# Hybrid two-layer trunk on one core: fewer diagonals ahead of the heads' square, one more attention level read by ScalarE, three convolution taps on TensorE, and the first norm's weights spread by TensorE

## The reference

```python
h = rmsnorm(x, ln1_w[l])
z = h @ w_in[l]                       # q, k, v, g, gate rank 16, ca, cb
o = gla_chunked(q * 64**-0.5, k, v, log_sigmoid(gate) / 16)   # 4 heads
o = rmsnorm(o, gla_norm_w) * silu(g)
u = causal_dwconv(ca * sigmoid(cb), conv_w, conv_b)  # 31 taps, 512 channels
u = silu(layernorm(u, cn_w, cn_b))
x = x + concat([o, u]) @ w_out[l]
h = rmsnorm(x, ln2_w[l])
x = x + (swiglu(h) if l == 0 else moe_swiglu(h))     # dense, then top 2 of 8
```

## Time and profile before

| what | value |
|---|---|
| median of the runs | 1262.99 us |
| the profiled execution's own time | 1263.23 us |
| its span (first to last instruction) | 1261.1 us |
| TensorE busy | 1220.4 us (97%) |
| VectorE busy | 1009.9 us (80%) |
| ScalarE busy | 815.5 us (65%) |
| mean granted TensorE clock | 0.993 of full |

### The profile page before, as it was taken

How to read it: one execution, slowest core, us unless ns; L and a number is a source line. 1 busy time by engine, 2 the same in 40 slices (tenths; PEclk the granted TensorE clock), 3 DMA queues, 4 the chain that set the end, 5 groups by cost and what they waited for, 6 DMA issues and landing times.

```text
span 1261.1 us, 16917 instructions
## 1 busy us (share of the span) xinstructions
PE 1220.4 (97%) x6868; PEld 1048.5 (83%) x6868; DVE 1009.9 (80%) x956; ACT 815.5 (65%) x725; POOL 58.9 (5%) x76
## 2 busy tenths in 40 slices
PE   8997999999999899999999999999999999999996
PEld 7986899999899678788888888888888888888875
DVE  5998475544579967888888888888888888888987
ACT  5854554443366645677777777777777777777775
POOL 4000000000000000000000000000000000000000
PEclk9999999999999998999999999999999999999999
DMA  9940465656536136999999999999999999999980
GB/s 278 351 133 17 151 196 173 198 174 194 167 134 235 51 123 240 355 368 365 375 388 366 378 384 367 382 383 365 380 385 363 376 388 364 381 385 359 396 319 35
DMA packets 182381, 360.11 MB, mean 286 GB/s; under 512 B 8926, under 2 KB 68636, under 8 KB 182300
## 3 DMA queue, kind: packets, MB, share of 16 engines
q1 hardware_dynamic: 178124, 343.77, 76.4%
q0 software_dynamic: 4176, 15.21, 3.2%
HBM read 351.09 MB, written 7.86 MB: 285 GB/s over the span
## 4 chain that ended last, share of the span: by engine, by line
PE 85%; DVE 9%; issue 2%; ACT 2%; SPq 1%; DMA 1%; DVEq 0%; ACTq 0%
PE YB L1838 17%; PE WBS L1817 13%; PE WBS L1819 12%; PE WBS L1818 12%; PE YB L1492 5%; PE WBS L1423 4%; PE WBS L1425 4%; PE WBS L1424 4%; DVE acc L924 3%; DVE w_lo L863 2%; PE YB L1829 2%; PE YB L1475 2%; PE YB L1853 2%; PE WBS L1581 1%; DMA raw<-in_w_in 1%
## 5 line engine op out<-in xcount | busy, mean ns | idle before, releaser
L863 DVE TENSOR_TENSOR w_lo<-raw,w_hi 128x2048 fp32r<-128x2048 f32 x324 | 736.8, 2289 | 110.1 <-ACT w_hi L533 107.5
L533 ACT ACTIVATE w_hi<-raw 128x2048 fp32r<-128x2048 f32 x324 | 617.1, 1916 | 144.9 <-PE YB L1838 62.1
L1817 PE MATMUL WBS<-w_hi,t_hi 128*128 128x512 f32 (+1 forms) x768 | 290.2, 378 | 1.8 <-DVE w_lo L863 1.8
L1819 PE MATMUL WBS<-w_hi,t_lo 128*128 128x512 f32 (+1 forms) x768 | 285.9, 372 | 0.0
L1818 PE MATMUL WBS<-w_lo,t_hi 128*128 128x512 f32 (+1 forms) x768 | 285.4, 372 | 0.0
L1817 PEld LDWEIGHTS WBS<-w_hi,t_hi 128*128 128x128 f32 x768 | 144.7, 188 | 26.7 <-issue 2.0
L1819 PEld LDWEIGHTS WBS<-w_hi,t_lo 128*128 128x128 f32 x768 | 144.6, 188 | 25.8
L1818 PEld LDWEIGHTS WBS<-w_lo,t_hi 128*128 128x128 f32 x768 | 144.8, 189 | 24.2
L1423 PE MATMUL WBS<-t_hi,w_lo 128*128 128x256 f32 x448 | 127.4, 284 | 0.0
L1424 PE MATMUL WBS<-t_hi,w_hi 128*128 128x256 f32 x448 | 126.8, 283 | 0.0
L1425 PE MATMUL WBS<-t_lo,w_hi 128*128 128x256 f32 x448 | 126.7, 283 | 0.0
(11 more groups left out here) (296 smaller groups left out, 1382.2 us busy)
## 6 DMA issues: line engine op xcount, KB each, us to landing
raw<-in_we_gate SPq DMA_DIRECT2D x88, 1024.0 KB, 6.7
raw<-in_we_up SPq DMA_DIRECT2D x88, 1024.0 KB, 6.9
raw<-in_we_down SPq DMA_DIRECT2D x88, 1024.0 KB, 6.8
raw<-in_w_in SPq DMA_DIRECT2D x20, 1024.0 KB, 5.9
raw<-in_wd_gate SPq DMA_DIRECT2D x11, 1024.0 KB, 5.5
raw<-in_wd_up SPq DMA_DIRECT2D x11, 1024.0 KB, 5.3
raw<-in_wd_down SPq DMA_DIRECT2D x11, 1024.0 KB, 4.9
raw<-in_w_out SPq DMA_DIRECT2D x8, 1024.0 KB, 8.0
```

The costliest lines, as they stand in the source:

```text
L533: act.activation(w_hi[:, hi_slot(n), :], raw[slot][:], ACT.Copy).then_inc(hi_ready, 1)
L863: dve.tensor_tensor(w_lo[slot][:], raw[slot][:], w_hi[:, hi_slot(n), :].bitcast(F32), ALU.subtract).then_inc(lo_ready, 1)
L1817: pe.matmul(bank, xs_hi[:, k0 + k, :], hi[:, k, :], start=start, stop=False)
L1819: ins = pe.matmul(bank, xs_lo[:, k0 + k, :], hi[:, k, :], start=False, stop=stop)
```

## The change

1. **Diagonals.** ScalarE makes 7 diagonals before the heads' square where it made 13, so the rest is made after it.
2. **Level 3** (blocks of 16) is read out by ScalarE, in 8 instructions of 16 partitions, after the high part of unit 13; VectorE's two instructions go. Levels 4 to 8 are read by one VectorE instruction each, which spans both banks.
3. **Taps.** `BY_VECTOR` goes from 27 to 24: three taps per layer move to TensorE, which now has 38. It makes 15 rather than 14 between the heads' outputs and the transposes, and 7 rather than 5 after them.
4. **First norm.** GpSimd's queue fetches one row of weights; TensorE spreads it over 128 partitions as a product with a row of ones into PSUM, VectorE reads it there. Fewer unread products precede it. GpSimd clears `lnw` afterwards.
5. **Router.** The first quarter of the logits is made between the two halves of the last output product.

```diff
-        COARSE, FINE = 3, 6
-        COARSE_READS = [2, 4, 8]
+        COARSE, FINE = 4, 5
+        COARSE_READS = [2, 4, 8, 16]
...
-        BY_VECTOR = 27
+        BY_VECTOR = 24
...
-                if t == 0:
-                    sp.dma_start(lnw[:], ln1_w[0].partition_broadcast(P)).then_inc(first_lnw_ready, 16)
...
+
+            pool.dma_start(lnw[0:1, :], ln1_w[0:1, :]).then_inc(first_lnw_ready, 16)
...
+                if l == 0:
+                    pool.wait_ge(first_lnw_spread, 2)
+                    pool.memset(lnw[:], 0.0).then_inc(pads_ready, 1)
...
+                coarse(3)
                 diagonals(3)
                 decays(7)
...
-                diagonals(13)
+                diagonals(7)
...
-                if t == 0:
-                    dve.wait_ge(lnw_ready if j else first_lnw_ready, 16 * max(j, 1))
-                dve.scalar_tensor_tensor(out=h[:, t, :], in0=X[:, t, :], scalar=rstd[:, t:t + 1], in1=lnw[:],
+                if j == 0:
+                    dve.wait_ge(first_lnw_spread, 2)
+                elif t == 0:
+                    dve.wait_ge(lnw_ready, 16 * j)
+                weights = lnw[:] if j else YB[:, 2:4, :].rearrange("p a c -> p (a c)")
+                dve.scalar_tensor_tensor(out=h[:, t, :], in0=X[:, t, :], scalar=rstd[:, t:t + 1], in1=weights,
...
-                        dve.wait_ge(level_read, 2 * (FINE * l + n - COARSE))
-                    for r in range(2):
-                        bank = YB[:, 2 * (n % 2) + r, :]
-                        ins = dve.copy_predicated(att[:, r], masks[:, n - 1:n, :].broadcast_to([P, 2 * TT, P]),
-                                                  bank.rearrange("p (a i) -> p a i", i=P))
-                        ins.then_inc(level_read, 1)
+                        dve.wait_ge(level_read, FINE * l + n - COARSE)
+                    bank = 2 * (n % 2)
+                    dve.copy_predicated(att[:].rearrange("p r a i -> p (r a) i"), masks[:, n - 1:n, :].broadcast_to([P, 4 * TT, P]),
+                                        YB[:, bank:bank + 2, :].rearrange("p r (a i) -> p (r a) i", i=P)).then_inc(level_read, 1)
...
-                level_read_out(3)
...
+                    if half:
+                        logits(0, 0)
...
-                    for t, count in ((0, 12), (1, 2)):
+                    def unread_ones(count):
                         for _ in range(count):
-                            pe.matmul(YB[:, 3, 0:P], ident[:], ones[:], start=True, stop=True)
-                        turn_h(0, t)
-                    for _ in range(3):
-                        pe.matmul(YB[:, 3, 0:P], ident[:], ones[:], start=True, stop=True)
+                            pe.matmul(YB[:, 1, 0:P], ident[:], ones[:], start=True, stop=True)
+
+                    unread_ones(2)
+                    pe.wait_ge(first_lnw_ready, 16)
+                    for half in range(2):
+                        cols = slice(HALF * half, HALF * (half + 1))
+                        pe.matmul(YB[:, 2 + half, :], ones[0:1, :], lnw[0:1, cols], start=True, stop=True).then_inc(first_lnw_spread, 1)
+                    unread_ones(2)
+                    turn_h(0, 0)
+                    unread_ones(4)
+                    turn_h(0, 1)
+                    unread_ones(3)
...
-                conv(14)
+                conv(15)
...
             turn_x(1, [0])
-            pe.wait_ge(router_ready, 1)
-            logits(0, 0)
             turn_x(1, [1])
```

More of the change, by code:

```diff
@@ L231, in trunk @@
         x_ready = [sem(f"x_ready{t}") for t in range(TT)]
-        first_lnw_ready = sem("first_lnw_ready")
+        first_lnw_ready, first_lnw_spread = sem("first_lnw_ready"), sem("first_lnw_spread")
         rows_ready, lnw_ready = sem("rows_ready"), sem("lnw_ready")
@@ L462, in _ @@
                 if l:
-                    pool.wait_ge(pads_ready, 2 + 3 * l)
+                    pool.wait_ge(pads_ready, 3 + 3 * l)
                     for k in range(2 * TT):
@@ L646, in mixer @@
                 act.activation(qk[:, 0].rearrange("p k t -> p (k t)"), in_bank("K"), ACT.Copy).then_inc(qk_ready, 1)
-                act.wait_ge(pads_ready, 3 * (l + 1))
+                act.wait_ge(pads_ready, 3 * (l + 1) + 1)
                 v_half(0)
@@ L1533, in turn_x, with logits @@
                     ins.then_inc(x_turned, 1)
+            def logits(t, g):
+                if (t, g) == (0, 0):
+                    pe.wait_ge(router_ready, 1)
+                pe.wait_ge(xT_ready, 2 * t + g + 1)
+                for k in range(4 * g, 4 * g + 4):
+                    ins = pe.matmul(YB[:, 0, NE * t:NE * (t + 1)], xT[t][:, P * k:P * (k + 1)], rt[:, k, :],
+                                    start=(k == 0), stop=(k == KD - 1))
+                return ins
             def turn_h(j, t):
@@ L1594, in level @@
                     elif n >= 2:
-                        pe.wait_ge(level_read, 2 * (FINE * l + n - 1 - COARSE))
+                        pe.wait_ge(level_read, FINE * l + n - 1 - COARSE)
                     if n == 0:
@@ L1661, in mixer @@
                 pe.wait_ge(coarse_read, COARSE_READS[-1] * (l + 1))
-                pe.wait_ge(level_read, 2 * FINE * (l + 1))
+                pe.wait_ge(level_read, FINE * (l + 1))
                 pe.wait_ge(og_ready, 2 * (l + 1))
@@ L1740, in _ @@
             mixer(1)
-            def logits(t, g):
-                pe.wait_ge(xT_ready, 2 * t + g + 1)
-                for k in range(4 * g, 4 * g + 4):
-                    ins = pe.matmul(YB[:, 0, NE * t:NE * (t + 1)], xT[t][:, P * k:P * (k + 1)], rt[:, k, :],
-                                    start=(k == 0), stop=(k == KD - 1))
-                return ins
             def unread(count):
```

2 lines of the change are left out of this document (1 added, 1 removed).

## The result

The changed kernel takes 1249.8 us, the median of four runs between 1249.21 and 1250.32, against 1262.78 for the kernel before beside it. The ratio is 0.9898, 95% interval 0.9881 to 0.9915. The forecast of 1252.1 is 2.3 us too slow, and the time lies just under the lower end of its range (1250.0). The profiled execution took 1250.32 us (span 1248.5), the one of before 1263.23.

A forecast was written before the change was run, and what follows sets the result against it. TensorE, busy 97% of the span, bounds the kernel, so only its waits pay. Start 1.2, layer 0 4.9, clock 1.65, layer 1 3.65, router -0.5: 10.9 us off 1263.2 gives 1252.3 profiled, 1252.1 median; range 1250.0 to 1256.8.

The forecast's parts named there:

- Start: Start of the kernel: the 512 KB broadcast leaves the transfer queue, 1.2 us gained, bounds 0 and 1.4.
- rival of the late row: Start: the row lands at 8 us or more, TensorE comes 3 us late to level 0; 1254.3 us, chance 0.11.
- Copies: Mixers: VectorE loses level 3's two copies and joins the other levels' pairs; 1.6 us in layer 0, 0.35 in layer 1.
- slow form: Mixers: the wide masked copy takes 7.0 us instead of 1.24; kernel about 1310 us, chance 0.04.
- Square: Both mixers: ScalarE's square starts when the heads' outputs end, so VectorE's wait before the sum of squares goes, 2.3 us each.
- New wait: Both mixers: the high part starts 1.0 us behind the transposes and VectorE waits for it, -0.5 us each.
- Taps: Both mixers: VectorE has 2 taps instead of 5 before the convolution's last addition, 1.5 us gained each.
- rival of the diagonals' pace: Both mixers: taps 22 to 30 run as round trips with their diagonals and hold the transposes; 1257.6 us, chance 0.10.
- Router: Router: the logits' quarter moves in front and TensorE then waits about 0.5 us; -0.5 us, bounds -0.8 and 0.
- Clock: Layer 0's mixer: TensorE's idles shrink, 2.4 GHz expected throughout; 1.65 us gained, bounds 0 and 1.65.
- sign of being wrong: Dense mixer: if it does not start 9 us earlier or so, the forecast is wrong.
- the clock stays low: Mixers: the 1.65 us loss stays in layer 0 (1253.8 us) or comes in layer 1 too (1255.4); chance 0.20.

The follow-up runs named there:

- u_start2: Changed kernel with its start undone (512 KB broadcast, 12 unread products ahead of the transposes), no tensor added: 1251.23 us, ratio 0.9912.
- row_first: Changed kernel with the row of norm weights issued first on SyncE's queue instead of GpSimd's: 1251.04 us, ratio 0.9911.
- p_diag: Kernel before with one edit, 7 instead of 13 diagonals ahead of the heads' square: 1258.76 us, ratio 0.9968.
- p_taps: Kernel before with one edit, three more taps per layer on TensorE: 1260.36 us, ratio 0.9976.
- b_keep_clock: Kernel before with unread products in the two places of each mixer where TensorE stands idle for VectorE: 1260.33 us, ratio 0.9984.
- p_logits: Kernel before with one edit, the first quarter of the logits between the halves of the last output product: 1263.02 us, ratio 1.0008.
- router_fill: Changed kernel with one unread product of 512 columns before each of the last three quarters of the logits: 1251.41 us, ratio 0.9915.

## Why the prediction was wrong, point by point

- **Start, booked 1.2 (0 to 1.4).** Right as far as single profiles tell: 1.34 by u_start2, 0.8 to 1.5 with their scatter. The norm is 1.9 us later than the 8.2 that I allowed it, because the row released TensorE 4.9 us behind its issue (1.36 to 6.23) and not at 4.6. The rival of the late row came half true, TensorE 0.87 later to level 0; what it cost is what row_first gets back, 0.35 us by the pair.
- **Copies, booked 1.6 and 0.35.** 1.13 (with 1.34 for the start) and 0.18 in the pair, 1.42 alone. One start-up saved per copy was worth 0.02, not 0.07: a narrow pair already ran in 1.22 from start to start. The slow form did not come.
- **Square, booked 2.3 twice.** Right: 2.40 and 2.39, and p_diag alone shows it.
- **New wait, booked -0.5 twice.** -0.14 and -0.13. ScalarE came as forecast, but VectorE's six taps (3.08 us) covered it. In p_taps the half microsecond is there only in layer 0, where the clock was low.
- **Taps, booked 1.5 twice.** Right: 1.57 and 1.56. The rival of the diagonals' pace is refuted: TensorE waits for them once per layer, 0.33 us. Its price was wrong besides: a loss of 6.4 us from the forecast of 1252.1 makes 1258.5, not 1257.6.
- **Layer 1, booked 3.65.** 3.98, by the smaller new wait.
- **Router, booked -0.5.** Right: -0.62 alone, and -0.65 in the pair.
- **Clock, booked 1.65, bounds 0 and 1.65. This step failed.** "Of the two stretches 0.9 + 0.75 = 1.65 us of work at 2.4 GHz was lost" is right as far as it goes: 1.60 in the pair, and b_keep_clock gets the same by keeping TensorE busy. But these were not the only stretches at 1.2 GHz, and the term for the router's clock stood at nothing without a reason. Between 470 and 490 us the trace of before lost 3.4 us' worth, half of which was not lost in the profiled execution after: of the 12.64 us 1.4 came there (12.64 - 11.87 + 0.65; 14.30 against 12.89 from the reduction on). The upper bound of 1.65 held for one place, and I let it stand for the kernel. That the clock falls less there is nothing that the change is shown to cause.
- **A sign of being wrong, misplaced.** I asked for a dense mixer that starts 9 us earlier or so, where my own sum gives 7.75; it starts 7.89 earlier.

The terms without the clock add up to 9.25 in the forecast (10.9 - 1.65) and to 9.62 in the pair (12.64 - 1.60 - 1.42); against b_keep_clock's profile they are 9.04, and at equal mean clock the runs give 8.5 to 10.4. So the steps on waits and work were right to half a microsecond in the traces and to about one in the runs, and most of the miss of 2.3 us is the clock. In the profiled execution (1250.32 for 1252.3) some 1.4 is the router's clock, 0.3 the other terms, and 0.25 lies outside the span (1.85 us around it, 2.1 before). Another 0.3 is the median, which lies 0.5 under the profiled execution, since two of the four runs had the highest clock, where I had allowed 0.2. Over all 14 runs the median of 1251.8 lies 0.3 from the forecast, but the range was drawn as if the clock could cost nothing beyond layer 0: its lower end had no room for the changed kernel's runs at the highest mean clock (0.998), 1249.3.

The rival "the clock stays low" was tied to the idles of the mixers. The Trainium skill (TensorE: Matmul & The Clock Gate, Part 1), on which I leaned there, says that an idle array is throttled. Layer 0 agrees in the main (1.00 when the idle places are filled, and a higher mean clock in all those runs, though p_logits had 1.00 there unfilled); the router does not: TensorE was busy 10.00 of 10 us where the clock was 0.74. Much of what is busy there is narrow, products of 8 columns and single transposes, but in both traces of the pair the clock fell among the nine wide products that follow them, and filling in three more wide ones did not help (router_fill). What decides about the router's clock stays open.

## What to carry to other kernels

Before booking a gain of clock, list the granted clock over the whole span, with each place below 1.00 and its worth, and give the time a range that holds both all of it and none of it; then compare runs of two kernels at an equal mean clock. An engine that makes something ahead for another should make no more than has a free buffer, if its next instruction is what a third engine waits for. And an experiment must add no tensor in the middle of the memory's layout, unless a kernel with only that tensor runs beside it.

## What the runs showed of the hardware that was not expected

- Four bytes more per partition ahead of the operand of the down products made each of them 4 to 5 ns longer (390 to 395, 401 to 406 ns at 512 columns) and the kernel 4.9 us slower at a mean clock of 0.998 (1254.2, one run, against 1249.3) and at 0.994 (1258.1, one run, against 1253.2). Neither the reason nor the best placement was looked for.
- The granted clock falls where TensorE shows no idle time, and in different places in executions of one kernel: between 460 and 470 us 0.83 and 0.58 in the changed kernel, and 1.00 in row_first, whose router is the same.
- A row of 4 KB issued by GpSimd at 1.36 us released TensorE at 6.23. Issued first by SyncE it was no longer what was waited for at 3.15.
